# Triangular substitution with one fused multiply-add per chunk and step, and its blocks loaded in two halves

## The reference, cut to what matters

```python
L = jnp.where(strict, jnp.einsum('bhncd,bhnjd->bhncj', k_beta, k) * decay, 0.0)
a = L + jnp.eye(C, dtype=jnp.float32)
rhs = jnp.concatenate([v * beta[..., None], k_beta * jnp.exp(gc)[..., None]], axis=-1)
sol = lax.linalg.triangular_solve(a, rhs, left_side=True, lower=True)
...
y = jax.nn.sigmoid(gr) * (o_r @ w_up_r) + jax.nn.sigmoid(gd) * (o_d @ w_up_d)
return x + y @ w_o
```

## Time and profile before

| what | value |
|---|---|
| median of 3 runs | 2684.73 us (2683.73 to 2685.75) |
| the profiled execution, its own time | 2687.57 us |
| its span in the profile | 2685.8 us |
| PE busy | 2643.1 us, 98% |
| DVE busy | 1726.8 us, 64% |
| ACT busy | 679.4 us, 25% |
| POOL busy | 826.2 us, 31% |

### The profile page before, as it was taken

How to read it: one execution, slowest core, us unless ns; L and a number is a source line. 1 busy time by engine, 2 the same in 40 slices (tenths; PEclk the granted TensorE clock), 3 DMA queues, 4 the chain that set the end, 5 groups by cost and what they waited for, 6 DMA issues and landing times.

```text
span 2685.8 us, 39894 instructions
## 1 busy us (share of the span) xinstructions
PE 2643.1 (98%) x14850; PEld 2259.3 (84%) x14850; DVE 1726.8 (64%) x3856; ACT 679.4 (25%) x1367; POOL 826.2 (31%) x455
## 2 busy tenths in 40 slices
PE   8899999999999999999999999999999999999998
PEld 6788888888888899888878888888888998898886
DVE  7778777777756555534577777778777555553333
ACT  5232323232312222200142333333332221230001
POOL 3223232323212112434422323233333122233443
PEclk9999999999999999999999999999999999999999
DMA  4322222222221112433532222222222111133344
GB/s 170 96 69 68 73 79 68 69 69 83 65 57 45 41 35 69 130 94 121 164 95 72 82 65 69 72 76 72 64 76 72 50 50 42 40 104 102 94 141 141
DMA packets 288484, 217.83 MB, mean 81 GB/s; under 512 B 31426, under 2 KB 245780, under 8 KB 288036
## 3 DMA queue, kind: packets, MB, share of 16 engines
q1 hardware_dynamic: 252322, 152.78, 20.3%
q10 hardware_dynamic: 35970, 62.50, 6.8%
HBM read 176.37 MB, written 38.86 MB: 80 GB/s over the span
## 4 chain that ended last, share of the span: by engine, by line
PE 89%; DVE 4%; DMA 3%; issue 2%; POOL 1%; SPq 1%; ACT 1%; DVEq 0%; ACTq 0%; POOLq 0%
PE dense_ps L773 22%; PE dense_ps L777 21%; PE dense_ps L775 21%; PE work L756 3%; PE dense_ps L797 2%; PE dense_ps L798 2%; PE dense_ps L799 2%; DMA arena<-l_scratch 1%; PE work L1028 1%; PE work L987 1%; PE work L1065 1%; PE work L1004 1%; PE work L1085 1%; PE work L1024 1%; PE work L1054 1%
## 5 line engine op out<-in xcount | busy, mean ns | idle before, releaser
L773 PE MATMUL dense_ps<-act_hi,w_hi 128*128 128x512 f32 x2560 | 1052.3, 411 | 2.8 <-POOL act_lo L2375 2.2
L777 PE MATMUL dense_ps<-act_hi,w_lo 128*128 128x512 f32 x2560 | 1002.4, 392 | 0.0
L775 PE MATMUL dense_ps<-act_lo,w_hi 128*128 128x512 f32 x2560 | 1000.9, 391 | 0.0
L2354 POOL TENSOR_TENSOR w_lo<-w_raw,w_hi 128x1024 fp32r<-128x1024 f32 x162 | 399.7, 2467 | 1018.5 <-ACT w_hi L1299 574.5
L777 PEld LDWEIGHTS dense_ps<-act_hi,w_lo 128*128 128x128 f32 x2560 | 481.1, 188 | 107.0
L773 PEld LDWEIGHTS dense_ps<-act_hi,w_hi 128*128 128x128 f32 x2560 | 483.2, 189 | 86.2 <-issue 3.1
L775 PEld LDWEIGHTS dense_ps<-act_lo,w_hi 128*128 128x128 f32 x2560 | 483.5, 189 | 79.6 <-issue 0.5
L1790 DVE SCALAR_TENSOR_TENSOR arena<-arena,cols 128x512 f32<-128x512 f32 x288 | 242.9, 843 | 5.1
L1299 ACT ACTIVATE w_hi<-w_raw 128x1024 fp32r<-128x1024 f32 x88 | 92.7, 1054 | 328.3 <-PE dense_ps L777 310.5
L1289 ACT ACTIVATE arena<-dense_ps 128x512 f32<-128x512 f32 x96 | 57.2, 596 | 264.0 <-PE dense_ps L777 264.0
L756 PE MATMUL work<-mk,arena 128*128 128x128 f32 x768 | 113.2, 278 | 8.5 <-issue 7.5
(11 more groups left out here) (239 smaller groups left out, 4037.0 us busy)
## 6 DMA issues: line engine op xcount, KB each, us to landing
w_raw<-in_w_in SPq DMA_DIRECT2D x140, 512.0 KB, 3.9
arena<-l_scratch SPq DMA_DIRECT2D x32, 512.0 KB
gate_scratch<-arena ACTq DMA_DIRECT2D x64, 256.0 KB, 2.2
arena<-gate_scratch ACTq DMA_DIRECT2D x64, 256.0 KB, 2.8
w_raw<-in_w_out SPq DMA_DIRECT2D x18, 512.0 KB, 3.7
o_scratch<-arena ACTq DMA_DIRECT2D x32, 256.0 KB, 2.0
w_raw<-in_w_up_dn SPq DMA_DIRECT2D x16, 512.0 KB, 3.7
arena<-o_scratch ACTq DMA_DIRECT2D x32, 256.0 KB, 3.5
```

What stands on the lines that cost most here:

```text
L773: eng.matmul(dense_ps[:, to, :], w_hi[:, slot, k, :], hi[:, k, seg], start=(k == 0), stop=False)
L775: eng.matmul(dense_ps[:, to, :], w_hi[:, slot, k, :], lo[:, k, seg], start=False, stop=False)
L777: mm = eng.matmul(dense_ps[:, to, :], w_lo[:, slot, k, :], hi[:, k, seg], start=False, stop=(k == KT - 1))
L2354: eng.tensor_tensor(w_lo[:, slot, :, :], w_from[second][:, :, :], w_hi[:, slot, :, :].bitcast(F32), ALU.subtract)\
```

## The change

Each step of the solve becomes four instructions, one for each chunk c. Each computes `xs[:, c, k+1:] = column * xs[:, c, k] + xs[:, c, k+1:]` in one operation (SCALAR_TENSOR_TENSOR), with `xs[:, c, k]` as a scalar of each partition. It waits for the same chunk's instruction of the step before, which is the fourth instruction ahead. `xm` is not used any more. A solve has 60 instructions where it had 30, and `sv_s` counts to 60.

The l load is issued in two halves of 256 KB, chunks 0 and 1 and then chunks 2 and 3, both from SP, except in the opening unit. There SP issues the first half, and ACT issues the second in its step "start", behind the activation and two waits. The solve starts when both halves have landed. GR0's load in the opening unit is no longer issued by SP behind the l load; ACT issues it in its step "kc", behind L1464.

```diff
-        nl_ok, sv_s = signal("neg_l_ready", 1), signal("solve_steps", 2 * BASE - 2)
-        l_st, l_in = signal("l_blocks_stored", 16 * NB), signal("l_blocks_loaded", 16)
+        nl_ok, sv_s = signal("neg_l_ready", 1), signal("solve_steps", CPH * (BASE - 1))
+        l_st, l_in = signal("l_blocks_stored", 16 * NB), signal("l_blocks_loaded", 32)
...
-        def l_source():
+        def l_source(c):
 
-            return l_dram[:, :, :, :].rearrange("a c i k -> a (c i k)").unsqueeze(1)\
-                .to_broadcast([NB, BASE, CPH * BASE * BASE])
+            return l_dram[:, c:c + 2, :, :].rearrange("a c i k -> a (c i k)").unsqueeze(1)\
+                .to_broadcast([NB, BASE, 2 * BASE * BASE])
...
-                    eng.dma_start(lb[:, :, :], l_source()).then_inc(l_in.sem, 16)
+                    for c in range(0, CPH if u else 2, 2):
+                        eng.dma_start(lb[:, c:c + 2, :], l_source(c)).then_inc(l_in.sem, 16)
...
-                load_w(n + BLK_FIRST + 3, w_src(l, w_in, GR0))
...
+                            if kind == "first":
+                                eng.wait_ge(l_st.sem, l_st.after(tn, 16 * NB))
+                                eng.wait_ge(sv_s.sem, sv_s.after(tn, 0))
+                                eng.dma_start(lb[:, 2:CPH, :], l_source(2)).then_inc(l_in.sem, 16)
                         elif what == "kc":
...
+                            if kind == "first":
+                                eng.wait_ge(w_lo_ok.sem, w_lo_ok.after(n + BLK_FIRST + 3, 0))
+                                eng.dma_start(w_raw[:, :, :], w_src(l, w_in, GR0)).then_inc(w_in_ok.sem, 16)
...
-                                eng.wait_ge(l_in.sem, l_in.after(tn, 16))
-                            else:
-                                eng.wait_ge(sv_s.sem, sv_s.after(tn, 2 * k))
-                            column = lb.rearrange("p c (i k) -> p c i k", i=BASE)[:, :, k + 1:BASE, k]
-                            eng.tensor_tensor(xm[:, :, 0:left], column, xs[:, :, k:k + 1].to_broadcast([P, CPH, left]),
-                                              ALU.mult).then_inc(sv_s.sem, 1)
-                            eng.wait_ge(sv_s.sem, sv_s.after(tn, 2 * k + 1))
-                            eng.tensor_tensor(xs[:, :, k + 1:BASE], xs[:, :, k + 1:BASE], xm[:, :, 0:left], ALU.add)\
-                               .then_inc(sv_s.sem, 1)
+                                eng.wait_ge(l_in.sem, l_in.after(tn, 32))
+                            column = lb.rearrange("p c (i k) -> p c i k", i=BASE)
+                            for c in range(CPH):
+                                if k:
+                                    eng.wait_ge(sv_s.sem, sv_s.after(tn, CPH * (k - 1) + c + 1))
+                                eng.scalar_tensor_tensor(out=xs[:, c, k + 1:BASE], in0=column[:, c, k + 1:BASE, k],
+                                                         scalar=xs[:, c, k:k + 1], in1=xs[:, c, k + 1:BASE],
+                                                         op0=ALU.mult, op1=ALU.add).then_inc(sv_s.sem, 1)
```

More of the change, by code:

```diff
@@ L2067, in delta_unit @@
                                 eng.wait_ge(xs_ok.sem, xs_ok.after(tn, 1))
-                                eng.wait_ge(l_in.sem, l_in.after(tn, 16))
-                            else:
-                                eng.wait_ge(sv_s.sem, sv_s.after(tn, 2 * k))
-                            column = lb.rearrange("p c (i k) -> p c i k", i=BASE)[:, :, k + 1:BASE, k]
-                            eng.tensor_tensor(xm[:, :, 0:left], column, xs[:, :, k:k + 1].to_broadcast([P, CPH, left]),
-                                              ALU.mult).then_inc(sv_s.sem, 1)
-                            eng.wait_ge(sv_s.sem, sv_s.after(tn, 2 * k + 1))
-                            eng.tensor_tensor(xs[:, :, k + 1:BASE], xs[:, :, k + 1:BASE], xm[:, :, 0:left], ALU.add)\
-                               .then_inc(sv_s.sem, 1)
+                                eng.wait_ge(l_in.sem, l_in.after(tn, 32))
[6 more added lines that the diff above has]
+                                                         op0=ALU.mult, op1=ALU.add).then_inc(sv_s.sem, 1)
                         elif what == "spread":
-                            eng.wait_ge(sv_s.sem, sv_s.after(tn, 2 * BASE - 2))
+                            eng.wait_ge(sv_s.sem, sv_s.after(tn, CPH * (BASE - 1)))
                             if t is not None:
```

## The result

The changed kernel takes 2691.06 us (median of 10 runs, 2687.82 to 2694.47); the kernel before, timed beside it, 2684.23. The ratio is 1.0024, 95% interval 1.0015 to 1.0033: 6.8 us slower, a loss of a quarter of a percent, with an interval that excludes no change. The forecast was 2688.6 us, with a range from 2674 to 2700. Timed once more, beside the kernels of the last group of experiments, the ratio was 1.0022 (1.0012 to 1.0031); one of its eleven runs took 6607 us and is left out of the ratio. The two profiled executions lie 3.3 us apart (spans 2685.8 and 2689.1 us). The execution profiled before lay 3.3 us above the median of its kernel (2687.57 against 2684.23), as the prediction said, and the one profiled after at its median (2690.90), which makes up the difference to 6.8.

The account below looks back on a forecast made before the run. PE, busy 98%, was taken to set the end, DVE costing time only where PE waits. Terms 9.9 - 2.8 - 0.9 - 2.3 = +3.9 us on 2687.57 gave 2691.5, on the medians 2688.6 us; range 2674 to 2700.

Parts of the forecast that it names:

- The fused instruction: DVE's solve: each instruction costs 0.124 us plus 1.3 ns a column, so a solve takes 8.06 us, 1.02 more.
- The rival with a free scalar: DVE's solve: a scalar costs nothing on few columns, 4.7 us a solve, about 11 us faster, 2673.7 us; chance 0.22.
- The waits: Fused solve: waits for the fourth instruction ahead are met; rival that they show, +10 ns giving about 2700.6 us, chance 0.17.
- The case without overlap: Fused solve: each instruction starts when the one ahead has ended, about 15 us a solve, over 2810 us; chance 0.05.
- The thirty later solves: Solves after each layer's first: L2091 comes 0.63 us later, delaying PE's L1065; +9.9 us in all.
- A punctual unit: Eighteen later solves that start on time: 0.50 us of cover against 0.63 us of delay, 2.3 us lost in all.
- The twelve late ones: Later solves where DVE waits for the l blocks: cover gone, 0.63 us lost each, 7.6 us in all.
- The halves: l load in two halves: smaller packets, half of a 0.37 us gain on 12 late solves, -2.3 us.
- The opening solves: First solve of each layer: GR0 earlier, less 1.02 us of longer solve, gives -1.7 and -1.1, -2.8 us in all.
- GR0's landing: Opening units: GR0's weights arrive 2.7 us earlier in layer 0 and 2.1 in layer 1, with half the l load ahead.
- The clock's term: PE behind the opening stalls: a shorter stall spares part of the half-speed clock, -0.9 us, between 0 and -1.8.
- The sum: Whole kernel: all terms together +3.9 us on the profiled execution, 2691.5 us, or 2688.6 us on the medians.

Follow-up runs that it names:

- the last group of experiments: Changed kernel, moved loads alone and two interleaved chains, timed beside the kernel before: 2691.92, 2675.45 and 2672.78 against 2685.99 us.
- the constant: Changed kernel with each fused instruction multiplying by the constant 0 instead of a scalar read from xs, blocks not inverted: 2667.68 us.
- that order: Changed kernel with each slot's twelve fused instructions ordered chunk by chunk, so two of three wait for the instruction just ahead: 3021.45 us.
- The second trace: Profiled execution of the unaltered changed kernel from its second timing beside the kernel before: span 2689.7 us; that timing's ratio 1.0022.
- the fused steps alone: Kernel before with only the fused solve, one l load and GR0 behind it on SP: 2701.78 us, ratio 1.0057 to the kernel before.
- the moved loads alone: Changed kernel with the old product and sum, keeping the l load's halves and GR0 from ACT: 2673.83 us, ratio 0.9956; later 2675.45, 0.9962.
- two interleaved chains: Moved loads with product and sum each cut into two alternating halves of the chunks: 2672.32 us, ratio 0.9948 to the kernel before; later 2672.78, 0.9950.
- the halves alone: Kernel before with only the l load in halves, the opening unit's second from ACT, GR0 on SP: 2678.55 us, ratio 0.9974.
- A count by two: Moved loads with fused steps in the two opening units only, the other thirty solves counting sv_s by two: 2722.17 us, 1.0135 times the kernel before.

## Why the prediction was right, step by step

**The fused instruction: right, and shown.** 0.124 us and 1.3 ns a column were forecast, 8.06 us a solve; measured were starts 0.13 us apart at one column and 0.15 at 15, and 8.39 us. The four L1987 were the right row to take. But the step from them has a slip: 0.26 less 128 columns at 1.04 ns is 0.127, not 0.124, and at the prediction's 1.2 us of span for a nanosecond the forecast should have been some 3 us higher. The rival with a free scalar gave 4.7 us a solve: the constant took 4.76 to its spread, so that rival had its size right for an instruction that reads no scalar. The rule of the Trainium skill beside it (Vector Engine (DVE) Microarchitecture Reference, Measured stream behaviour on trn2: about 75 ns after overlap plus 1.04 ns a column) fits the instruction with a constant, 0.07 to 0.09 us, and not the one with a scalar.

**The waits: right.** At a distance of four they are met. The Trainium skill's page VectorE: DVE Perf Modes says in its section The DRAIN you can't avoid, of eight copies that take 13.88 us, that a semaphore after each "costs nothing extra". Here, with short operations, a dependent neighbour starts 0.12 us later than an independent one, and some 330 us hang on that order; the measurement decides. The case without overlap, at 15 us a solve, is closest to this order (13.37).

**The thirty later solves: right in kind, and in size by luck.** 0.63 us later at L2091 was forecast; measured are 3.42 - 3.07 and 1.66 - 1.28, 0.73 us. What that costs PE was mis-sized both ways. A punctual unit was to lose 0.13 us, 18 of them 2.3; with the matmuls of the two traces matched one by one it loses 0.29 at L1065 (median), all 18 together 5.4. The twelve late ones were to lose 0.63 each less the halves' 0.19, 5.3 in all; they lost 1.7. The prediction took their cover to be gone, as in unit 9, but before the change PE waited at L1065 only 3 times (1.2 us), and its weight load 9 times. With 0.6 behind the last solves of the layers, PE fell behind by 7.7 us at L1065, beside a forecast of 9.9 - 2.3 = 7.6: two errors that cancel. The second trace has 9.5, the fused steps alone 11.5. And the prediction left out a place: L1024, behind the spread, comes 0.05 to 0.08 us later in each of the thirty units, 2.0 us in all.

**The halves: right way, too small.** The last landing of the l load came 6.8 us after its issue before (median of 32) and 5.9 us after the first half's issue now, 0.9 us sooner; the other kernels with halves have 6.0 to 6.3, those with one load 6.8. I had allowed 0.19 and had an end at 0.37. The packets' times alone don't give that; what else does was not tried apart.

**The opening solves: right way, mis-sized.** The two stalls at L1024 fell by 10.1 - 4.8 = 5.3 us, where the term was -2.8. The size that was off is GR0's landing: I had it come 2.7 us earlier, behind half of the l load; in fact it was issued ahead of the load, and DVE did not wait for it (0.82 us in the second trace). The clock's term was too small as well (-0.9, at most -1.8): it was priced by L987 alone, but the dense matmuls behind it run at the 1.2 GHz level too. With the matmuls matched one by one, what ran slowly behind the two stalls before the change cost 5.2 us; that much is regained by the moved loads alone, where the clock does not fall behind the stalls. The changed kernel regained 2.0 of it in the first trace and all 5.2 in the second. The mean granted clock behind its stall, 0.59, shows the 1.2 GHz level for most of the window in the first trace (views of windows: busy by engine, then the clock, of the changed kernel and of the moved loads alone):

```profile
88.00:92.00 4.00, 4.00 (x21) 3.61 (x20) 3.56 (x7) 0.63 (x1) 0.00 (x0) 0.59 0.00 0
```

The moved loads alone:

```profile
86.00:90.00 4.00, 3.64 (x25) 3.32 (x26) 3.93 (x8) 0.63 (x1) 0.00 (x0) 1.00 0.10 36
```

The second trace of the changed kernel:

```profile
88.00:92.00 4.00, 3.67 (x25) 3.32 (x26) 3.93 (x8) 0.63 (x1) 0.00 (x0) 1.00 0.00 0
```

PE's timeline of the second trace:

```profile
88.33 1.00 PE L1024 MATMUL work<-arena 128*112 128x64 f32 x8 [2.17 <-DVE arena L2088]
```

The moved loads alone, with a stall of 0.89 us, have 1.00, the 2.4 GHz level, throughout. The changed kernel's stall of 2.22 us in one trace and 2.17 in the other was followed by 0.59 and 1.00. I had let the loss shrink with the stall; between the two traces of the same code it differs by 3.2 us, and the stalls at L1024 by only 0.3. What decides it was not found.

**The sum: close, in part by luck.** Matched one by one, the opening units gave back 6.9 us (5.3 of stall, 2.0 of clock, less 0.3 lost again at L1041, where PE waits for DVE), where 2.8 + 0.9 = 3.7 were forecast. The later units cost 7.7 + 2.0 = 9.7, where 7.6 were forecast. That is +2.8 of the 3.3 us between the traces; the rest lies at lines of which the forecast does not speak. In the second trace it is 11.4 - 9.0 = +2.4 of 3.9. Both halves of the forecast's +3.9 were too small, and the errors cancel. The medians differ by 6.8 and 5.9, more than the traces, mostly because the execution profiled before lay above the medians of the kernel before, by 3.3 us in the first timing and 1.6 in the second. GR0's landing and the clock move by more than a microsecond between executions of the same code, so one pair of traces does not give such a difference more closely.

## What to carry to other kernels

- Price a small instruction by the spacing of starts in a row of its own kind, operands included. Halving the operations by fusing them brought twice the instructions, each with 0.06 us for its scalar, and the fused form lost 15 us where it had looked like less work.
- Where a chain of dependent small operations binds, look at the distance of its waits before its operations: two interleaved chains took 6.51 us for what one chain took 7.04 and the fused form 8.39.
- Time the parts of a change apart. Here a gain of 12.7 us was hidden in a change that lost 6.8.

## What the runs showed that I had not expected

**DVE and POOL in each other's way.** As soon as GR0 came earlier, one of the two DVE instructions that split it took about a microsecond longer: L1648 2.21 us in the changed kernel where L1641 has 1.23 us with the fused steps alone; L1642 1.84 us in the moved loads alone, where the changed kernel has 0.68. In the traces of these two kernels from the last group it is the other way round (L1642 1.56, and L1648 2.19). Each time a POOL instruction ran at that moment. POOL's timeline of the changed kernel:

```profile
75.22 1.68 POOL L2440 TENSOR_TENSOR arena<-arena,mk 128x512 f32<-128x512 f32 x1 [1.30 <-DVE arena L2024]
```

The moved loads alone:

```profile
74.85 1.29 POOL L2441 TENSOR_TENSOR arena<-arena,mk 128x512 f32<-128x512 f32 x1
```

In the kernel before and with the halves alone the split comes after POOL's instruction and takes 0.69 and 1.23 us. So about 1 us of each opening gain was given back. The Trainium skill, SBUF — State Buffer, section Who interferes with whom, has a rule that would explain it: a port pair that DVE and GpSimd share, which one instruction holds to its end while the other is blocked. The trace agrees roughly: L1648 ends 1.08 us after POOL's instruction does. It was seen in the kernels that issue GR0 ahead of the l load, and not isolated.

**A count by two.** Raising a semaphore by two in place of one made the waits instructions of their own and cost some 0.06 us on each instruction of the chain: 2722.17 - 2675.45 = 46.7 us over the moved loads alone, of which some 3 belong to the fused opening solves. No part of the change weighs as much.
